# Which token tile gets scattered gates, and in which order the seam asks for its tables: a deal of tiles and two hand-written schedules changed in a decoder layer with expert retrieval

## The chip, the cores and the metric

The kernel runs on one core of one Trainium2 chip. The metric is the device time of one execution in microseconds (us); lower is better. TensorE (PE) does the matrix products, VectorE (DVE) the ranking, the gathered rows and the additions, ScalarE (ACT) copies PSUM out and evaluates activations, GpSimd (POOL) issues the indirect transfers, and SyncE (SP) issues most of the others.

## The reference, cut to what matters

```python
h = concat([meta, x])                                  # 16 + 1024 rows of 1024
proj = rmsnorm(h, norm_mix_g) @ w_in                   # 1024 -> 2048
ya = rmsnorm(pool_mixer(a, pool_w, pool_scale), norm_a_g)
yb = rmsnorm(short_conv_mixer(b_gate, c_gate, val, conv_w), norm_b_g)
h = (h + concat([ya, yb]) @ w_out)[:, 16:]
xf = rmsnorm(h, norm_ffn_g)
# retrieval: 8 heads, 2 x 128 sub-keys, top 16 of each half, top 16 of their sums
idx, gates = peer_retrieve(xf, w_query, sub_keys)      # (1024, 8, 16): expert numbers below 16384
u, v = expert_u[idx], expert_v[idx]
h = h + sum_k gates_k * gelu(u_k . xf) * v_k           # 128 experts for each token
return rmsnorm(h, norm_final_g)
```

## The kernel before

The 1024 tokens are eight tiles of 128. They go through the mixer and the ranking in four groups of two tiles, in the order of `BASE`. A tile's place in that order is its *rank*, 0 to 7. The expert part is then done in two ways:

- Four tiles are **gathered**: for each of 128 choices POOL issues one indirect transfer of 128 rows of 4 KB from `expert_u` (a *row* below, line 626), and DVE takes the dot product (L1122). Later the same is done with `expert_v` (L1133). The rows go through a ring of 8 slots. There are 1024 rows in all, of which the first 256 are the u rows of the first two gathered tiles.
- Four tiles are **dense**: PE multiplies them with all of `expert_u` (`score_tile`, L733, 128 tiles x), ACT applies gelu (L929), DVE multiplies by a table of gates (a *gate* item, L1185), and PE multiplies the result with `expert_v` (L779, 16 groups of 8 pieces), which DVE adds up (a *sum* item, L1191). The tables lie in `g_d`. For three of the dense tiles they are made on chip from one-hot products in 48 batches (`hots`, L1335 and L1339 on DVE, L746 on PE) and stored in chunks (L538). For the fourth, POOL scatters the gates into the table in HBM: 128 indirect transfers, 16 for each of 8 heads (L597). A head's transfers are issued once those of the head before have landed. I call them *scatters*.

The stages follow one another on PE: group n's projections (`bcv`), the output product (`outp`, L691), the turn (L697), the queries and the scores; after group 3 the stage of table batches, with ten score tiles in it and behind it; then the *seam*, where the first sums begin; then the dense stage proper.

The order of DVE's work is written by a small planner. `FILL` gives each slot of a group (behind each convolution, behind `outp`, in the query stage) a budget in us, and `take` fills it with ranking units of the group before (`keys`, `cands`, `pairs`, `digits`, `pick`, `keep`) and with rows of tiles already ranked. `plan["hots", b]` puts rows beside the table batches. What remains is merged with the dense items into `order`: `first_fill` is the place at which gate items begin, and `DENSE_SPEED` their pace. `digits` on DVE releases `pick_places` on ACT (L812, 16 activations), and `pick` waits for it. POOL works through its rows in order, and `head_after` says after which row the scatters of each head stand.

Before, ranks 0, 1, 6 and 7 are gathered, rank 2 is scattered, and ranks 3, 4 and 5 get tables. The scatters stand behind rows 29 (heads 0 and 1), 37 (heads 2 to 4) and 45 (heads 5 to 7). PE's steps don't depend on this deal.

## Time and profile before

| | before |
|---|---|
| median of 3 runs | 2651.85 us (2648.74 to 2654.02) |
| profiled execution, its own time | 2652.4 us |
| its span, first to last instruction | 2650.7 us |
| PE busy | 2509.4 us (95%) |
| DVE busy | 1953.4 us (74%) |
| POOL busy | 1436.2 us (54%) |
| ACT busy | 430.6 us (16%) |
| mean over the span | 324 GB/s |

1.7 us of the profiled time lie outside the span. Times of rows below are counted from the start of the span. "Idle before" in a row is the time for which the engine did nothing ahead of that instruction, and behind the arrow stands who ended it.

### The profile page before, as it was taken

The page shows a single profiled execution, that of the slowest core. Times are in us where ns is not written, and L with a number is a line of the kernel's source. Part 1 is how long each engine was busy: PE and PEld are TensorE (multiplying, and loading weights), DVE is VectorE, ACT ScalarE, POOL GpSimd, SP SyncE. Part 2 cuts the span into 40 slices and gives each one's busy share as a digit, 9 for nine tenths or more (in the row PEclk, how much of TensorE's full clock was granted, in tenths as well). Part 3 has the DMA queues.
Part 4 walks back from the last instruction along what each step waited for, and adds up shares of the span by engine and source line. Part 5 has one row for each costly group of instructions (what it writes and reads, how often), then busy time and mean ns, then how long its engine had stood idle before and what let it go on. Part 6 is the DMA issues. An engine that isn't in the chain of part 4 may idle for free.

```text
span 2650.7 us, 24105 instructions
## 1 busy us (share of the span) xinstructions
PE 2509.4 (95%) x7657; PEld 1380.6 (52%) x7657; DVE 1953.4 (74%) x4210; ACT 430.6 (16%) x790; POOL 1436.2 (54%) x1169
## 2 busy tenths in 40 slices
PE   8999999998878899999999999999999999999993
PEld 7687785876756344444444444444444444444441
DVE  3207678668669788686988867769787687877878
ACT  1212223313678100100010100000000000001010
POOL 0000220678762256676756757657576675666665
PEclk9999999998999899999999999999999999999996
DMA  8543763666589979999999999999999999999998
GB/s 320 188 165 143 296 260 127 191 199 180 134 234 257 363 271 391 348 361 415 381 388 402 383 419 353 389 401 387 419 389 397 384 349 420 391 404 395 371 372 306
DMA packets 285918, 857.88 MB, mean 324 GB/s; under 512 B 41952, under 2 KB 97248, under 8 KB 271200
## 3 DMA queue, kind: packets, MB, share of 16 engines
q0 software_dynamic: 167184, 541.73, 54.8%
q1 hardware_dynamic: 108336, 289.45, 28.9%
q10 hardware_dynamic: 10272, 25.17, 2.4%
q8 instruction: 61, 1.00, 0.1%
q14 instruction: 65, 0.53, 0.1%
HBM read 807.94 MB, written 48.30 MB: 323 GB/s over the span
## 4 chain that ended last, share of the span: by engine, by line
PE 69%; POOL 11%; DVE 7%; DMA 5%; issue 4%; ACT 1%; DVEq 1%; another core or an unknown queue 0%; ACTq 0%; POOLq 0%
PE pairs L779 29%; PE pairs L733 27%; POOL gate_tables L597 8%; PE pairs L646 7%; POOL ring L626 4%; PE pairs L691 3%; DMA ring<-in_expert_u,idx 3%; PE pairs L665 2%; DVE arena L1339 1%; DMA gate_tables<-gate,place 1%; DVE junk L1122 1%; ACT pick_all L812 1%; DMA arena<-gate_tables 1%; PE pairs L658 0%; DVE work L1002 0%
## 5 line engine op out<-in xcount | busy, mean ns | idle before, releaser
L626 POOL DMA_INDIRECT ring<-in_expert_u,idx x512 | 650.8, 1271 | 575.7 <-DVE dots L1122 307.7
L779 PE MATMUL pairs<-arena 128*128 128x512 f32 x2048 | 885.5, 594 | 13.7 <-DVE arena L1185 11.2
L733 PE MATMUL pairs<-arena 128*128 128x512 f32 x2048 | 882.8, 592 | 3.8 <-ACT arena L929 3.8
L1122 DVE CUSTOM_DVE_ANT_0 junk<-ring,xf 128x1024 bf16<-128x1024 f32 x512 | 612.1, 1223 | 182.6 <-DMA ring<-in_expert_u,idx 177.2
L626 POOL DMA_INDIRECT ring<-in_expert_v,idx x512 | 567.0, 1107 | 326.4 <-DVE arena L1133 149.0
L779 PEld LDWEIGHTS pairs<-arena 128*128 128x128 f32 x2048 | 389.8, 191 | 506.9 <-issue 502.3
L733 PEld LDWEIGHTS pairs<-arena 128*128 128x128 f32 x2048 | 388.5, 190 | 490.5 <-issue 490.5
L1133 DVE SCALAR_TENSOR_TENSOR arena<-ring,arena 128x1024 f32<-128x1024 f32 x381 | 473.4, 1283 | 97.4 <-DMA ring<-in_expert_v,idx 92.3
L646 PE MATMUL pairs<-arena 128*128 128x256 f32 (+1 forms) x1792 | 403.3, 388 | 10.9 <-ACT arena L882 9.7
L646 PEld LDWEIGHTS pairs<-arena 128*128 128x128 f32 x1792 | 342.9, 192 | 69.2 <-ACT arena L882 10.3
L597 POOL DMA_INDIRECT gate_tables<-gate,place x128 | 211.7, 1654 | 166.0 <-DVE gate L1141 102.3
L929 ACT ACTIVATE arena<-pairs 128x512 f32<-128x512 f32 x128 | 76.1, 597 | 1197.5 <-PE pairs L733 1018.9
L1133 DVE SCALAR_TENSOR_TENSOR xf<-ring,arena,xf 128x1024 f32<-128x1024 f32 x126 | 155.6, 1283 | 13.9 <-DMA ring<-in_expert_v,idx 13.7
L746 PE MATMUL pairs<-arena 128*128 128x128 f32 x768 | 96.7, 285 | 37.4 <-DVE arena L1339 19.0
L1185 DVE TENSOR_TENSOR arena<-arena 128x512 f32<-128x512 f32 x128 | 87.5, 688 | 60.3 <-ACT arena L929 42.6
L691 PE MATMUL pairs<-arena 128*128 128x512 f32 x256 | 114.3, 605 | 4.0 <-ACT arena L860 4.0
L1191 DVE TENSOR_TENSOR arena<-arena,pairs 128x512 f32<-128x512 f32 x128 | 87.1, 681 | 40.1 <-PE pairs L779 27.9
L746 PEld LDWEIGHTS pairs<-arena 128*128 128x128 f32 x768 | 92.3, 199 | 44.8 <-DVE arena L1339 26.1
L1339 DVE TENSOR_SCALAR arena<-iota,arena 128x128 f32<-128x128 f32 x384 | 101.9, 356 | 8.5 <-PE pairs L746 8.4
L812 ACT ACTIVATE pick_all<-digit,place 128x256 bf16<-128x256 f32 x128 | 80.3, 725 | 81.6 <-DVE digit L1066 81.6
L691 PEld LDWEIGHTS pairs<-arena 128*128 128x128 f32 x256 | 49.5, 194 | 64.2 <-issue 56.6
L998 DVE MAX8 tops<-arena 128x8 f32<-128x128 f32 x112 | 24.5, 280 | 73.2 <-ACT arena L891 71.7
(160 smaller groups left out, 1088.4 us busy)
## 6 DMA issues: line engine op xcount, KB each, us to landing
arena<-in_w_all SPq DMA_DIRECT2D x80, 1024.0 KB
arena<-in_uT SPq DMA_DIRECT2D x128, 512.0 KB
arena<-in_expert_v SPq DMA_DIRECT2D x128, 512.0 KB
arena<-gate_tables SPq DMA_DIRECT2D x32, 1024.0 KB
gate_tables<-arena SPq DMA_DIRECT2D x12, 2048.0 KB
gate_tables<-junk ACTq DMA_DIRECT2D x4, 2048.0 KB, 13.8
ring<-in_expert_u,idx POOLq DMA_INDIRECT x512
ring<-in_expert_v,idx POOLq DMA_INDIRECT x512
```

Of the source, the lines that this page charges most:

```text
L597: nc.gpsimd.indirect_dma_start(out=g_flat, out_offset=bass.IndirectOffsetOnAxis(ap=place[:, k:k + 1], axis=0), in_=gate[:, k:k + 1], in_of ...
L626: nc.gpsimd.indirect_dma_start(out=ring[:, r % RING, :], out_offset=None, in_=expert_u if table == "u" else expert_v, in_offset=bass.Indir ...
L646: last = nc.tensor.matmul(out_, w[:, k, c * P:(c + 1) * P], xn[:, k, :], start=(k == 0), stop=(k == KD - 1))
L691: last = nc.tensor.matmul(pair[:, q * 512:(q + 1) * 512], yT[:, NG * (1 - half) + k, t * P:(t + 1) * P], w_out[q].rearrange("p k n -> p (k ...
L733: last = nc.tensor.matmul(score_bank[x], uslot[:, x % USLOTS, k * P:(k + 1) * P], xfT[:, k, :], start=(k == 0), stop=(k == KD - 1))
L746: last = nc.tensor.matmul(g_bank[(2 * b + m) % 4][:, q * KEYS:(q + 1) * KEYS], hots[:, c, 0, 4 * m + q, :], hots[:, c, 1, 4 * m + q, :], s ...
L779: last = nc.tensor.matmul(o_bank[n % 4], gated[:, x % GSLOTS, t * P:(t + 1) * P], vrows[:, j, half * 512:(half + 1) * 512], start=(j == 0) ...
L812: last = nc.scalar.activation(pick_hot[:, a], digit[:].rearrange("p h s k -> p k (h s)"), ACT.Square, scale=32.0, bias=place16[:, a:a + 1])
L1122: nc.vector.tensor_tensor_reduce(out=junk[:, r % 2, :], in0=row, in1=xf[:, t % 2, :], scale=1.0, scalar=0.0, op0=ALU.mult, op1=ALU.add, ac ...
L1133: nc.vector.scalar_tensor_tensor(out=to[:, k % 2, :], in0=row, scalar=weight[:, k:k + 1], in1=h2 if k == 0 else to[:, k % 2, :], op0=ALU.m ...
L1185: nc.vector.tensor_tensor(s, s, gtab[a // GJ % 2][:, :, a % GJ, :], ALU.mult).then_inc(w_ready, 1)
L1339: last = nc.vector.tensor_scalar(hots[:, c, 1, t, :], iota[:], routeT[:, 1, k:k + 1], routeT[:, 2, k:k + 1], ALU.is_equal, ALU.mult)
```

## The change

Two edits in one. The first deals the ranks out anew: rank 1 is scattered, 0, 3, 6 and 7 are gathered, 2, 4 and 5 get tables. The scatters thus stand behind row 29 (heads 0 to 3) and row 54 (heads 4 to 7), the budgets of `FILL` become one list for each group, and DVE takes 79 rows ahead of the final order, not 60: 22 in group 1, 25 in group 2 (before 8), 16 in group 3 (before 16), and 16 beside table batches (before 14), now from batch 2 on and not from batch 21. The second is about the seam: the last chunk of tables is stored in two transfers, the small first one with what tables 0 and 1 need of it; the load of table 0 waits for the small one only; the additions' starting values are loaded tile by tile ahead of four loads of u; gate items begin after two units of keys and six rows (before: after five units and 14 rows), eight in a row and not ten. `digits` is held back until three sums in a row follow, or until its `pick`.

```diff
-GATHERED_RANK = {0: 0, 1: 1, 6: 2, 7: 3}
-SCATTER_RANK = 2
-DENSE_RANK = {3: 0, 4: 1, 5: 2}
+GATHERED_RANK = {0: 0, 3: 1, 6: 2, 7: 3}
+SCATTER_RANK = 1
+DENSE_RANK = {2: 0, 4: 1, 5: 2}
...
-FILL = (("conv0", 4.0), ("conv1", 4.0), ("conv2", 4.0), ("conv3", 4.0), ("gate", 4.0), ("y", 15.0), ("outp", 10.0), ("query", 68.0))
+FILL = [[(f"conv{g}", 4.0) for g in range(4)] + [("gate", 4.0), ("y", 15.0), ("outp", outp), ("query", query)]
+        for outp, query in ((0.0, 0.0), (10.0, 70.0), (10.0, 72.0), (0.0, 72.0))]
-ROWS_FROM = 20
-FIRST_FILL = 54.0
+FIRST_FILL = 26.0
...
-            plan["hots", b] = take(HOT_FILL) if b >= ROWS_FROM and b % 2 == 1 else []
+            plan["hots", b] = take(HOT_FILL) if b % 3 == 2 else []
...
             if i == first_fill:
-                order += items[:EARLY]
-                done = EARLY
-            order.append(unit)
+                order += items[:VJ]
+                done = VJ
+            if unit[0] == "pick" and held:
+                order.append(held.pop())
+            if unit[0] == "digits":
+                held.append(unit)
+            else:
+                order.append(unit)
+            if held and done + 2 < len(items) and all(k == "sum" for k, _, _ in items[done:done + 3]):
+                order.append(held.pop())
...
-                sp.dma_start(g_d[:, :, FIRST_CHUNK + c, :].rearrange("g p n -> p g n"),
-                             tables[:, c % STAGES].rearrange("p (g j) t -> p g (j t)", j=GJ)).then_inc(table_kept[c % STAGES], 16)
+                if c < TABLE_CHUNKS - 1:
+                    sp.dma_start(to, of).then_inc(table_kept[c % STAGES], 16)
+                else:
+                    sp.dma_start(to[:, 0:2], of[:, 0:2]).then_inc(first_kept, 16)
+                    sp.dma_start(to[:, 2:], of[:, 2:]).then_inc(table_kept[c % STAGES], 16)
...
-            head_after = [scatter_from - 1 + RING * (1 + (h + 1) // 3) for h in range(HEADS)]
+            head_after = [rows_by[1 + 2 * h // HEADS] + RING - 1 for h in range(HEADS)]
```

**On POOL's queue**, from the middle of group 1 up to the table stage (`ring<-in_expert_u` are rows, `gate_tables<-gate` are scatters; the number behind x counts them). Before:

```order
L626 DMA ring<-in_expert_u,idx 128x1024 x30
L597 DMA gate_tables<-gate,place 8388608x1 x32
L626 DMA ring<-in_expert_u,idx 128x1024 x8
L597 DMA gate_tables<-gate,place 8388608x1 x48
L626 DMA ring<-in_expert_u,idx 128x1024 x8
L597 DMA gate_tables<-gate,place 8388608x1 x48
L626 DMA ring<-in_expert_u,idx 128x1024 x82
```

And of the changed kernel:

```order
L651 DMA ring<-in_expert_u,idx 128x1024 x30
L622 DMA gate_tables<-gate,place 8388608x1 x64
L651 DMA ring<-in_expert_u,idx 128x1024 x25
L622 DMA gate_tables<-gate,place 8388608x1 x64
L651 DMA ring<-in_expert_u,idx 128x1024 x73
```

Three blocks of scatters have become two of 64, each followed by rows that DVE takes in the query stage of a group.

**On DVE**, at the end of group 3's ranking and the start of the table stage. Before (`half_i` is the end of the last pick, `gsum` the sums for the gates that PE's first turn of routes waits for, the last two rows are batch 0):

```order
L1080 TENSOR_TENSOR half_i<-pick_all 128x16x8x2
L1101 COPY route<-half_i 128x2x128
L1102 TENSOR_TENSOR route<-best 128x128
L1137 TENSOR_REDUCE gsum<-route 128x8
L1139 RECIPROCAL gsum<-gsum 128x8
L1141 TENSOR_TENSOR route<-route,gsum 128x128
L1335 TENSOR_TENSOR arena<-iota,arena 128x1024
```

And of the changed kernel, where a row is the pair of instructions that reads `ring`, and eight such pairs stand where two are shown first and last:

```order
L1107 TENSOR_TENSOR half_i<-pick_all 128x16x8x2
L1128 COPY route<-half_i 128x2x128
L1129 TENSOR_TENSOR route<-best 128x128
L1149 ISA junk,dots<-ring,xf 128x1024
L1149 ISA dots 128x1
...
L1149 ISA junk,dots<-ring,xf 128x1024
L1149 ISA dots 128x1
L1164 TENSOR_REDUCE gsum<-route 128x8
L1166 RECIPROCAL gsum<-gsum 128x8
L1168 TENSOR_TENSOR route<-route,gsum 128x128
```

Eight rows, 55 to 62, have come in between the last ranking unit and the gates on which the table stage waits.

**On SP's queue** at the seam, from the last chunk of tables on. Before (`gate_tables<-arena` stores, `arena<-gate_tables` loads a table):

```order
L538 DMA gate_tables<-arena 128x32x128
L523 DMA arena<-in_expert_v 128x1024 x3
L528 DMA arena<-gate_tables 128x2048
L523 DMA arena<-in_expert_v 128x1024 x5
L528 DMA arena<-gate_tables 128x2048
L517 DMA arena<-in_uT 128x1024 x4
L554 DMA arena<-h_scratch 128x4x1024
L528 DMA arena<-gate_tables 128x2048 x2
```

And of the changed kernel:

```order
L553 DMA gate_tables<-arena 128x2x128
L554 DMA gate_tables<-arena 128x30x128
L533 DMA arena<-in_expert_v 128x1024 x3
L538 DMA arena<-gate_tables 128x2048
L533 DMA arena<-in_expert_v 128x1024 x5
L538 DMA arena<-gate_tables 128x2048
L575 DMA arena<-h_scratch 128x1024 x4
L527 DMA arena<-in_uT 128x1024 x4
L538 DMA arena<-gate_tables 128x2048 x2
```

The order of the loads of tables and of v is the same; the store is in two, and the starting values stand ahead of the loads of u.

## Rows read from the trace of the kernel before

**Rows 1.** Windows: busy us of PE, PEld, DVE, ACT, POOL; clock, DMA share, GB/s

```profile
1141.00:2604.70 1463.70, 1463.66 (x3410) 647.82 (x3410) 1154.76 (x1480) 92.59 (x149) 964.37 (x825) 1.00 0.99 388
```

**Rows 2.** The chain of work that ended last: start, us, what

```profile
2549.80 54.95 PE pairs L779 x128
```

**Rows 3.** Timeline of DVE, tail: start, us, instruction, operands, count

```profile
2608.48 34.72 DVE L1133 SCALAR_TENSOR_TENSOR xf<-ring,arena,xf 128x1024 f32<-128x1024 f32 x28
```

**Rows 4.** Timeline of PE, groups 2 and 3 and the table stage

```profile
416.82 15.11 PE L691 MATMUL pairs<-arena 128*128 128x512 f32 x28 [3.55 <-ACT arena L860]
...
577.04 13.90 PE L691 MATMUL pairs<-arena 128*128 128x512 f32 x32
...
615.93 1.94 PE L697 MATMUL pairs<-ident,arena 128*128 128x128 f32 x8 [7.80 <-DVE arena L1280]
...
695.29 7.40 PE L746 MATMUL pairs<-arena 128*128 128x128 f32 x48 [4.07 <-DVE arena L1339]
...
737.66 7.03 PE L733 MATMUL pairs<-arena 128*128 128x512 f32 x16
...
764.11 7.03 PE L733 MATMUL pairs<-arena 128*128 128x512 f32 x16
...
802.82 7.03 PE L733 MATMUL pairs<-arena 128*128 128x512 f32 x16
```

**Rows 5.** Timeline of DVE: rows that waited for their transfer, groups 1 and tables

```profile
366.56 1.23 DVE L1122 CUSTOM_DVE_ANT_0 junk<-ring,xf 128x1024 bf16<-128x1024 f32 x1 [2.48 <-DMA ring<-in_expert_u,idx]
...
775.25 1.22 DVE L1122 CUSTOM_DVE_ANT_0 junk<-ring,xf 128x1024 bf16<-128x1024 f32 x1 [15.95 <-DMA ring<-in_expert_u,idx]
```

**Rows 6.** Timeline of POOL: rows (L626) and scatters (L597)

```profile
344.05 1.69 POOL L626 DMA_INDIRECT ring<-in_expert_u,idx  x1 [19.67 <-DVE dots L1122]
346.05 1.99 POOL L626 DMA_INDIRECT ring<-in_expert_u,idx  x1 [0.31 <-issue]
...
355.21 1.49 POOL L626 DMA_INDIRECT ring<-in_expert_u,idx  x1 [0.30 <-issue]
...
368.06 0.95 POOL L626 DMA_INDIRECT ring<-in_expert_u,idx  x1 [1.92 <-DVE dots L1122]
471.28 1.63 POOL L597 DMA_INDIRECT gate_tables<-gate,place  x1 [102.27 <-DVE gate L1141]
...
507.56 2.44 POOL L597 DMA_INDIRECT gate_tables<-gate,place  x1 [5.02 <-DMA gate_tables<-gate,place]
...
768.30 1.00 POOL L626 DMA_INDIRECT ring<-in_expert_u,idx  x1 [0.31 <-issue]
```

**Rows 7.** Page, costliest groups: busy, mean ns of one; idle before

```profile
L597 POOL DMA_INDIRECT gate_tables<-gate,place x128 | 211.7, 1654 | 166.0 <-DVE gate L1141 102.3
```

**Rows 8.** Waits: us in total, times, longest

```profile
POOL gate_tables L597 <- DMA gate_tables<-gate,place: 26.5, 5, 7.5
```

**Rows 9.** Timeline of PE, the seam and the first tiles behind it

```profile
904.83 5.46 PE L779 MATMUL pairs<-arena 128*128 128x512 f32 x6 [11.05 <-DVE arena L1185]
...
1107.14 27.70 PE L733 MATMUL pairs<-arena 128*128 128x512 f32 x64 [3.77 <-ACT arena L929]
```

**Rows 10.** Timeline of DVE at the seam: keys, gates, a sum

```profile
860.48 0.86 DVE L998 MAX8 tops<-arena 128x8 f32<-128x128 f32 x4
...
869.41 0.68 DVE L998 MAX8 tops<-arena 128x8 f32<-128x128 f32 x3
...
906.71 2.50 DVE L1185 TENSOR_TENSOR arena<-arena 128x512 f32<-128x512 f32 x4 [0.19 <-DMA arena<-gate_tables]
923.09 1.30 DVE L1185 TENSOR_TENSOR arena<-arena 128x512 f32<-128x512 f32 x2 [13.88 <-DMA arena<-gate_tables]
...
951.13 0.68 DVE L1191 TENSOR_TENSOR arena<-arena,pairs 128x512 f32<-128x512 f32 x1
```

**Rows 11.** SP's queue at the seam: start, us, transfer

```profile
883.57 0.43 SPq L528 DMA_DIRECT2D arena<-gate_tables  x1
```

**Rows 12.** Windows around the seam's start, columns as in Rows 1

```profile
893.80:912.00 18.20, 7.17 (x10) 3.09 (x11) 14.79 (x50) 2.30 (x3) 6.18 (x5) 0.62 1.02 420
```

More of the change, by code:

```diff
@@ L255, in program @@
         kept = [sem(f"kept{i}") for i in range(GT)]
-        xfT_kept = sem("xfT_kept")
+        xfT_kept = [sem(f"xfT_kept{n}") for n in range(GRPS)]
         keyed = sem("keyed")
@@ L326, in ranking_of, with ranking_of_two @@
                     + [("digits", r, 0), ("pick", r, 0), ("keep", r, 0)])
-        def ranking_of_two(r):
+        def ranking_of_two(r, keys):
             one, two = ranking_of(r), ranking_of(r + 1)
-            return one[:8] + two[:2] + one[8:] + two[2:]
+            return one[:8] + two[:keys] + one[8:] + two[keys:]
         plan, to_rank, ranked = {}, [], set()
-        rows, row_limit, since_digits = 0, 2 * HK, 0.0
+        rows, since_digits = 0, 0.0
         def take(us):
-            nonlocal rows, since_digits, scatter_from, row_limit
+            nonlocal rows, since_digits
             got, spent = [], 0.0
@@ L510, in _ @@
             sp.wait_ge(pe_step, LAST_STEP)
-            sp.wait_ge(xfT_kept, 16 * len(DENSE_GROUP))
+            for n in range(GRPS):
+                if DENSE_OF[n]:
+                    sp.wait_ge(xfT_kept[n], 16 * len(DENSE_OF[n]))
             sp.dma_start(xfT, xfT_d).then_inc(xfT_in, 16)
@@ L549, in _ @@
                 load_v(0, j)
+            stage_kept(last_stage)
             load_gates(1)
+            for t in range(DENSE_TILES):
+                sp.dma_start(sums[:, t, :], of_tile(h2_d, DENSE_TILE[t])).then_inc(d_h2_in, 16)
             while next_u < EARLY + USLOTS:
@@ L572, in _ @@
                 sp.wait_ge(d_out, t + 1)
-                sp.dma_start(of_tile(out, t), sums[:, t, :]).then_inc(out_kept, 16)
+                sp.dma_start(of_tile(out, DENSE_TILE[t]), sums[:, t, :]).then_inc(out_kept, 16)
         @block.gpsimd
@@ L1324, in _ @@
             dve.wait_ge(act_emptied, ACT_STEPS)
-            dve.wait_ge(xfT_kept, 16 * len(DENSE_GROUP))
+            for n in range(GRPS):
+                if DENSE_OF[n]:
+                    dve.wait_ge(xfT_kept[n], 16 * len(DENSE_OF[n]))
             for t in range(GT):
```

67 lines of the change are left out of this document (37 added, 30 removed).

## The prediction

> **What bounds the kernel now.** I read the windows first. From 1141 us to 2604.7 us PE is busy for 1463.66 of 1463.70 us at full granted clock [rows 1], and the chain of waits runs through PE alone up to 2604.75 us [rows 2]. One item, a score tile or a piece of a sum, takes 54.95 / 8 = 6.87 us there. DVE is busy 79% of that stretch and waits for PE. So rows taken out of this stage bring nothing by themselves: their number shows only in the tail, where DVE works off 28 rows that stand behind the last sum, 34.72 us or 1.24 us each [rows 3]. The end is therefore the start of PE's unbroken stretch plus a constant, and what can move is PE's idle time before 1141 us. The timeline of PE shows it, and each stall names who was late:
> - Group 2's output product stalls for 3.55 us because DVE came late from group 1's rows; group 3's turn stalls for 7.80 us [rows 4].
> - The table stage has a steady beat of one score tile and eight batches: 764.11 - 737.66 = 26.45 us. The next beat takes 802.82 - 764.11 = 38.71 us [rows 4]. The reason is on DVE: row 46 came 15.95 us late [rows 5], because POOL issued it at 768.30, behind all scatters [rows 6]. That costs 38.71 - 26.45 = 12.3 us.
> - At the seam PE stands for 11.05 us for the first gate item, and 3.77 us at 1107 us, where ACT's gelu was behind the 16 activations for a `pick` [rows 9].
>
> **The change, part by part.** PE's own instructions are the same. The two new DMA issues on SP and one more on ACT for the tile-wise `xfT` cost some 0.5 us of their queues (0.43 us for one at the seam [rows 11]); I count them at nothing.
>
> *The scatters and the rows behind them.* All of this is POOL's chain, worked out step by step. A scatter takes 1.654 us [rows 7] and 0.3 us to the next; 64 make 125.1 us. Between two heads lies a wait for landing, 26.5 / 5 = 5.3 us [rows 8]; three make 15.9 us. A block of four heads is 141.0 us. The first block starts when row 29 is out: 368.06 + 0.95 [rows 6], plus 1.0 us for the longer `keep` of a scattered rank, so at about 370.3 us, not at 471.28. It ends at 511.3 us, about when the picks of group 2 are done. Then row 30 goes out, and DVE has 17 rows to take. With DVE idle a row's issue takes 0.95 + 0.3 = 1.25 us, and with DVE at rows 1.99 + 0.3 = 2.29 us [rows 6]; the 14 of group 1 took 24.0 us for 13 steps, 1.85 us each. Six at 1.25 and ten at 1.85 put row 46 at 537.3 us. From issue to use it takes 7.0 us in a quiet stretch (768.30 to 775.25) and 11.4 us while weights are loaded (355.21 to 366.56) [rows 5, 6]; I take 9. So group 2's rows end at 547.5 us.
>
> Then row 54 can be issued, and the second block runs from 548.8 to 689.8 us. Behind it stand rows 55 to 62, which DVE must have before the gates that the table stage waits for. The last goes out ten us later (five at 1.25, two at 1.85), lands 7 us after that and is used by 708.0 us; one us for the gates makes 709.0 us. Before, PE had its first routes turned at 691.2 us (695.29 - 4.07 [rows 4]); half a us of that is the turning itself. So the table stage starts **18 us later**: the wait that stood at 759 us has moved to 690 us.
>
> Whether PE or DVE would be later still must be asked. After group 1's rows PE's stall ended 416.82 - 367.8 = 49.0 us behind the last row [rows 4, 5]. From 547.5 that gives 596.5 us in group 3, where PE stood at 577.0 us [rows 4], now 1 us later: up to 18.5 us lost, of which 7.8 us come back, since `keys` and `pick` have left the slot ahead of the turn. PE is ready some 12 us late, at 703 us, still ahead of 709. So that stall is hidden behind POOL's chain; with a quicker POOL it would come out.
>
> *The table stage itself.* Its rows now find a full ring: **-12.3 us**. Two rows more stand there. A beat has 2.7 rows at 1.2 us beside DVE's work for eight batches, which with four rows before took no longer than PE's 26.45, so they are hidden. Only the row in batch 2, where PE is still waiting for DVE at the start (4.07 us [rows 4]), is on the path: **+1.2 us**.
>
> *The seam.* Write P for the shift so far, +6.9 us; the times here are without it. DVE reaches the gate items after two units of keys and six rows, 2 x 8.93 us [rows 10], some 25 us sooner than before, and must now wait for the tables. Table 0 is asked for before the big store lands. Table 1 is not: it was asked for at 883.57 [rows 11] and used at 906.71 [rows 10], 23 us later, in queues full at 420 GB/s [rows 12]. It can't be asked for before about 881. What is ahead of it is the same, but a DVE that waits draws no rows. The bounds are 892 (all of the band for it) and 906.7; I take 898. So gates 4 to 7 are done at 900.5 us. PE, free at 893.8, goes through four products and waits little. But now the units of keys stand between gates and sums: two units, six rows, two gates, one more unit and two rows, 27.7 us with the first sum, and some 1.8 us for table 2, which took 13.88 us of waiting before [rows 10]. First sum at 930; the next three come at 8.4, 8.4 and 9.6 us, each longer than PE's 6.87, so the fourth at 956.4. PE needs one more piece: 963.3 us. Before, it was the third sum at 951.13 + 0.68 [rows 10] and two pieces, 965.5 us. **-2.2 us** only. The 11.05 us are mostly turned into waits for the four sums. Half a clock for some us is in the old figure (0.62 granted in that window [rows 12]) and in mine is hidden behind DVE.
>
> *Digits held back.* The 16 activations now stand where PE is at sums and needs no new gelu: **-3.8 us** [rows 9]. DVE waits some 10 us for them, with 27 us of PE's pieces as cover; without it the 10 us would be PE's.
>
> *The tail.* 27 rows, not 28: **-1.2 us**.
>
> Sum: 18.0 + 1.2 - 12.3 - 2.2 - 3.8 - 1.2 = -0.3 us on the profiled 2652.4 us, which stands 0.5 us above the median of the runs. So about **2651 us**.
>
> **A rule weighed against the trace.** A row's issue takes 0.95 us with DVE idle and 1.99 us with DVE at rows [rows 6]. The Trainium skill, "SBUF — State Buffer", section "SBUF: two separate sides", says that a DVE operation with two SBUF inputs and a GpSimd operation that reads SBUF take a shared port pair in turns, and the later one stands until the other is done. By that rule all rows behind DVE's would cost the long price; the trace has a mean of 1.85, since DVE itself often waits for a row. By the one the sum is as above, by the other it is the rival D below.
>
> **The rivals.**
> - *A, as forecast*: the scatters' wait moves ahead and eats what the table stage gives. 2651 us. For it: the same 128 scatters at a fixed rate, and rows behind them in front of the gates.
> - *B, POOL is quicker*: landing waits of half the size and rows that land in 7 us. The first block saves 8, the rows 2; group 2's rows end at 537.5 us, the second block at 672 us, and POOL is no longer late. PE's own stall is then 537.5 + 49.0 - 578 = 8.5 less 7.8 us, and DVE's ranking, with one unit and one pick more in the query slot, some us: +5 for +18. The time is 2638 us. Against it: five waits with a mean of 5.3 us.
> - *C, the seam gives what it promises*: table 1 at 892 and no wait for table 2: first sum at 922, PE hardly stands, and the seam gives 10 us, not 2.2. 2643 us. Against it: the band was full.
> - *D, slower*: every row of the two runs behind the scatters is issued at 2.29 us and lands in 11.4. Group 2's rows end 4.4 + 2.4 = 6.8 us later, the last of group 3 another 0.9 + 4.4 us. The table stage starts 18 + 12 = 30 us late. 2663 us. It decides from a start about 24 us late.
>
> **How the numbers follow.** What a measurement of this kernel can tell from no change is about 0.2%, 5.3 us. A has 0.38, B 0.26, C 0.15, D 0.21. A lies inside the 5.3 us on both sides, so: faster 0.40 (B, most of C), same 0.38, slower 0.22. The range takes B and C in and D up to its nearer part: 2636 to 2662 us. Within A alone it is 2646 to 2657 us.
>
> **What the profile of the changed kernel would show.** POOL: scatters in two blocks, from about 370 to 511 and from 549 to 690 us. PE: a stall of ten us or more at group 3's output product, none of 7.8 us at its turn, then some ten us ahead of the turn of routes, waiting for DVE's gates, and there DVE waiting for rows. In the table stage, every beat 26.45 us. At the seam no idle of 11 us, but short waits for DVE's sums (L1191 before), 5 us at the first. No 3.77 us in the tiles behind group 1. A tail 1.2 us shorter. I am wrong if POOL's second block ends before 675 us, or if gates 4 to 7 are done well before 900 us on the old clock.

## The result, and the profile after

| | before | changed |
|---|---|---|
| median of the runs, us | 2653.81 | 2660.59 |
| fastest and slowest run, us | 2644.22, 2657.03 | 2655.36, 2668.75 |
| runs | 11 | 11 |

The ratio is 1.0033, with a 95% interval of 1.0023 to 1.0043: the change makes the kernel slower by a third of a per cent, 8.8 us. (The medians in the table are 6.8 us apart and the means 9.0; 8.8 is the ratio applied to the median of before.) The ratios leave out slow executions, of which there was one (6661 us, of the kernel with 51 early rows below). The profiled execution of the changed kernel took 2665.74 us (span 2664.0), 13.3 us over that of before. A second profile of it in a later group of runs had a span of 2656.7 us; the ratio there was 1.0044 (1.003 to 1.0058).

Windows of the changed kernel over the stretch of [rows 1], columns as there:

```profile
1141.00:2604.70 1463.70, 1457.12 (x3391) 644.82 (x3390) 1130.32 (x1455) 101.50 (x163) 947.55 (x803) 1.00 0.97 380
```

PE is still busy nearly throughout, but 6.5 us less than in [rows 1]: there is a stall that was not there before. The chain of waits again ends with PE alone, and the last piece starts 14.5 us later than in [rows 2]:

```profile
2564.30 54.95 PE pairs L804 x128
```

So the loss arose earlier. PE's timeline, with the places of [rows 4] and [rows 9] and some new ones (L804 is the sum, L779 before; L758 the score tile, L733 before; L771 the table batch, L746 before; L716 the output product, L691 before; L671 the query, L646 before):

```profile
15.90 17.89 PE L690 MATMUL pairs<-arena 128*128 128x272 f32 x64 [3.21 <-DVE arena L1236]
...
303.19 1.19 PE L671 MATMUL pairs<-arena 128*128 128x256 f32 x2 [10.10 <-ACT arena L907]
...
476.57 2.05 PE L671 MATMUL pairs<-arena 128*128 128x256 f32 x4 [4.59 <-ACT arena L907]
...
599.09 3.52 PE L716 MATMUL pairs<-arena 128*128 128x512 f32 x4 [2.71 <-ACT arena L885]
...
712.50 0.87 PE L748 MATMUL pairs<-ident,route 128*128 128x128 f32 x3 [10.07 <-issue]
717.44 7.64 PE L771 MATMUL pairs<-arena 128*128 128x128 f32 x48 [4.07 <-DVE arena L1368]
...
761.26 7.03 PE L758 MATMUL pairs<-arena 128*128 128x512 f32 x16
...
787.69 7.03 PE L758 MATMUL pairs<-arena 128*128 128x512 f32 x16
...
877.44 27.63 PE L758 MATMUL pairs<-arena 128*128 128x512 f32 x64
...
975.90 55.10 PE L758 MATMUL pairs<-arena 128*128 128x512 f32 x128
...
1140.70 27.63 PE L804 MATMUL pairs<-arena 128*128 128x512 f32 x64
1174.91 29.79 PE L804 MATMUL pairs<-arena 128*128 128x512 f32 x64 [6.58 <-DVE arena L1218]
1204.53 5.74 PE L758 MATMUL pairs<-arena 128*128 128x512 f32 x13
```

The same rows of before that [rows 4] lacks:

```profile
14.93 14.90 PE L665 MATMUL pairs<-arena 128*128 128x272 f32 x64 [3.21 <-DVE arena L1209]
...
866.15 27.63 PE L733 MATMUL pairs<-arena 128*128 128x512 f32 x64
...
1134.69 6.17 PE L779 MATMUL pairs<-arena 128*128 128x512 f32 x14
...
1190.04 10.46 PE L733 MATMUL pairs<-arena 128*128 128x512 f32 x24
```

In before, the first score tile behind the seam starts at 965.70 us, group 2's sums at 1134.69 and the tiles behind them at 1190.04; in the change these are 975.90, 1140.70 and 1204.53. Read by stages, against the forecast's terms:

| stretch | forecast, us | profiles, us |
|---|---|---|
| start of the tables | +18.0 | 717.44 - 695.29 = +22.2 |
| table stage | 1.2 - 12.3 = -11.1 | (877.44 - 717.44) - (866.15 - 695.29) = -10.9 |
| seam, to the first whole score tile | -2.2 | (975.90 - 877.44) - (965.70 - 866.15) = -1.1 |
| tiles behind group 1 | -3.8 | (1140.70 - 975.90) - (1134.69 - 965.70) = -4.2 |
| sums of group 2 | 0 | (1204.53 - 1140.70) - (1190.04 - 1134.69) = +8.5 |
| tail, behind PE's last piece | -1.2 | 13.3 - 14.5 = -1.2 |

These make the +13.3 of the two profiled executions. Some 4 us of the first line are no effect of the change: 64 matmuls at 15.90 us took 17.89 us where the same ones of before took 14.90, and group 0's scores, ahead of all that the change moves, begin at 188.98 us against 185.12. The change's second profile has 16.59 us there, and its tables start at 710.98 us. With these 4 us out, the 13.3 become about 9, and the runs say 8.8. The first line has one more disturbance, on the other side. Ahead of group 1's query the profile of before stands 5.97 us, of which some 3 are a wait of ACT for which it names no engine ("3.22 <-remote" at 291.14 below); the profiles of the kernels further down that store behind both copies have 1.7 to 2.3 us at this place. The first profile of the change has such a wait too (3.17 us at 294.95), its second has not. Counted from group 0's first query, the tables start 695.29 - 128.43 = 566.9 us on in before, and 717.44 - 132.28 = 585.2 and 710.98 - 129.72 = 581.3 us on in the two profiles of the change. So the line is +14 to +18 us with the start taken out.

Two new stalls stand out, and the profile shows the cause of each. The first is on ACT, at the end of group 1's turns. L907 copies a turn to the buffer that PE's query reads; L911 stores the transposed tile, L872 and L873 store two others. Columns: start, us, instruction.

```profile
294.95 1.02 ACT L907 ACTIVATE arena<-pairs 128x1024 f32<-128x1024 f32 x1 [3.17 <-remote]
296.01 0.55 ACTq L911 DMA_DIRECT2D xfT_scratch<-arena  x1
296.59 0.85 ACTq L872 DMA_DIRECT2D h_scratch<-arena  x1
297.47 4.55 ACTq L873 DMA_DIRECT2D xf_scratch<-arena  x1
302.07 1.02 ACT L907 ACTIVATE arena<-pairs 128x1024 f32<-128x1024 f32 x1 [6.09 <-issue]
```

The copy of the second turn starts 6.09 us after ACT could have had it, and what fills the time are three issues on its own queue, one of them of 4.55 us. The stores of h and xf stand between the two copies in the kernel before as well. But there they are issued while the first copy runs; only the store of the transposed tiles, which waits for a copy to end, stands behind both:

```profile
291.14 1.02 ACT L882 ACTIVATE arena<-pairs 128x1024 f32<-128x1024 f32 x1 [3.22 <-remote]
291.15 0.33 ACTq L847 DMA_DIRECT2D h_scratch<-arena  x1
291.51 0.53 ACTq L848 DMA_DIRECT2D xf_scratch<-arena  x1
294.08 1.02 ACT L882 ACTIVATE arena<-pairs 128x1024 f32<-128x1024 f32 x1 [1.91 <-remote]
295.13 0.59 ACTq L886 DMA_DIRECT2D xfT_scratch<-arena  x1
```

Five more profiles, of kernels below that keep this order of stores, have 10.24 to 10.52 us ahead of group 1's query. There the first copy has no such wait, and the stores of h and xf behind the transposed tile take 1.31 to 1.66 and 6.58 to 7.04 us. In group 2 they take 1.43 to 1.81 and 0.53 to 0.84 us in all six.

The second is on DVE, in the sums of group 2 (L1149 is a row, L1092 and L1093 the end of the digits, L1099 the start of the pick, L1218 a sum):

```profile
1147.02 1.23 DVE L1149 CUSTOM_DVE_ANT_0 junk<-ring,xf 128x1024 bf16<-128x1024 f32 x1 [1.28 <-DMA ring<-in_expert_u,idx]
...
1151.82 0.28 DVE L1093 TENSOR_TENSOR digit<-pos,pick_all 128x128 f32<-128x128 uint32 x1
1162.12 2.29 DVE L1099 TENSOR_TENSOR pick_all<-topf,pick_all 128x4096 bf16<-128x4096 bf16 x1 [10.02 <-ACT pick_all L837]
...
1174.17 0.69 DVE L1218 TENSOR_TENSOR arena<-arena,pairs 128x512 f32<-128x512 f32 x1
```

The digits end at 1152.1, DVE waits 10.02 us for ACT's 16 activations, and behind the waiting pick stand two rows, a gate, three rows and the first sum. PE has nothing to do without that sum: it stands for 6.58 us, and the 64 matmuls behind the stall take 29.79 us instead of 27.63.

### The profile page after: what moved, and what is told of

Read it like the earlier page. It is cut to its first block, busy times and chain, and to the rows that moved or that the text cites. A ratio compares the mean times of both kernels' runs of the same rounds, so it can differ in the third digit from the quotient of the medians.

```text
span 2664.0 us, 24115 instructions
## 1 busy us (share of the span) xinstructions
PE 2521.2 (95%) x7657; PEld 1388.3 (52%) x7657; DVE 1954.5 (73%) x4210; ACT 430.1 (16%) x790; POOL 1430.7 (54%) x1169
## 4 chain that ended last, share of the span: by engine, by line
PE 69%; POOL 11%; DMA 7%; issue 5%; DVE 4%; ACT 3%; ACTq 1%; DVEq 0%; another core or an unknown queue 0%; POOLq 0%; SPq 0%
PE pairs L804 28%; PE pairs L758 28%; POOL gate_tables L622 7%; PE pairs L671 7%; DMA ring<-in_expert_u,idx 4%; POOL ring L651 4%; PE pairs L716 2%; PE pairs L690 2%; DMA gate_tables<-gate,place 1%; ACT arena L948 1%; PE pairs L771 1%; ACT arena L972 1%; DVE junk L1149 1%; ACT pick_all L837 1%; DMA arena<-gate_tables 1%
## 5 line engine op out<-in xcount | busy, mean ns | idle before, releaser
L651 POOL DMA_INDIRECT ring<-in_expert_u,idx x512 | 636.1, 1242 | 685.8 <-DVE dots L1149 410.0
L804 PE MATMUL pairs<-arena 128*128 128x512 f32 x2048 | 891.0, 597 | 15.3 <-DVE arena L1218 12.0
L758 PE MATMUL pairs<-arena 128*128 128x512 f32 x2048 | 882.5, 592 | 0.0
L651 POOL DMA_INDIRECT ring<-in_expert_v,idx x512 | 578.7, 1130 | 330.0 <-DVE arena L1160 166.4
L1149 DVE CUSTOM_DVE_ANT_0 junk<-ring,xf 128x1024 bf16<-128x1024 f32 x512 | 613.4, 1224 | 179.8 <-DMA ring<-in_expert_u,idx 165.7
L804 PEld LDWEIGHTS pairs<-arena 128*128 128x128 f32 x2048 | 391.7, 192 | 512.2 <-issue 496.4
L758 PEld LDWEIGHTS pairs<-arena 128*128 128x128 f32 x2048 | 388.6, 190 | 486.5 <-issue 486.5
L671 PE MATMUL pairs<-arena 128*128 128x256 f32 (+1 forms) x1792 | 406.5, 390 | 18.3 <-ACT arena L907 16.5
L671 PEld LDWEIGHTS pairs<-arena 128*128 128x128 f32 x1792 | 344.9, 193 | 77.6 <-ACT arena L907 17.1
L1218 DVE TENSOR_TENSOR arena<-arena,pairs 128x512 f32<-128x512 f32 x128 | 87.2, 682 | 49.9 <-PE pairs L804 32.2
L771 PE MATMUL pairs<-arena 128*128 128x128 f32 x768 | 94.0, 282 | 28.9 <-ACT arena L972 22.8
L716 PE MATMUL pairs<-arena 128*128 128x512 f32 x256 | 114.9, 607 | 5.1 <-ACT arena L885 5.1
L771 PEld LDWEIGHTS pairs<-arena 128*128 128x128 f32 x768 | 91.1, 197 | 34.8 <-issue 24.5
L716 PEld LDWEIGHTS pairs<-arena 128*128 128x128 f32 x256 | 49.7, 195 | 65.6 <-issue 56.1
```

The lines of the kernel that those rows point to most:

```text
L651: nc.gpsimd.indirect_dma_start(out=ring[:, r % RING, :], out_offset=None, in_=expert_u if table == "u" else expert_v, in_offset=bass.Indir ...
L671: last = nc.tensor.matmul(out_, w[:, k, c * P:(c + 1) * P], xn[:, k, :], start=(k == 0), stop=(k == KD - 1))
L716: last = nc.tensor.matmul(pair[:, q * 512:(q + 1) * 512], yT[:, NG * (1 - half) + k, t * P:(t + 1) * P], w_out[q].rearrange("p k n -> p (k ...
L758: last = nc.tensor.matmul(score_bank[x], uslot[:, x % USLOTS, k * P:(k + 1) * P], xfT[:, k, :], start=(k == 0), stop=(k == KD - 1))
L771: last = nc.tensor.matmul(g_bank[(2 * b + m) % 4][:, q * KEYS:(q + 1) * KEYS], hots[:, c, 0, 4 * m + q, :], hots[:, c, 1, 4 * m + q, :], s ...
L804: last = nc.tensor.matmul(o_bank[n % 4], gated[:, x % GSLOTS, t * P:(t + 1) * P], vrows[:, j, half * 512:(half + 1) * 512], start=(j == 0) ...
```

## The experiments

My theory after the result: the loss is these two waits. The forecast had seen both instructions, had counted the stores at nothing and the wait of the pick as covered by other work. The rivals: the later start of the tables is a matter of POOL's chain, as forecast; or the early rows are not worth what they cost. In all runs the ratio is to the kernel before, measured on the same chip and in the same group of runs. The change itself came out at 1.0033 above and at 1.0044 in the last group, so a difference of 0.1% across groups says nothing.

**The two edits apart.** The first kernel has the new deal of ranks alone, with the seam's instructions as before; the second the old deal with the seam's edit.

> The first edit alone: the new deal of tiles, POOL's two blocks of scatters, the new budgets and rows beside table batches, with the seam, the start of the gate items and the place of digits as before. Theory: this edit is itself a loss. In the changed kernel's profile the table stage ended at 877.4 us, before at 866.2; some 4 us of these 11 are a slower start of that one execution (the same instructions of group 0 ended 4 us later), 7 us are the edit's. The 3.77 us at the tiles behind group 1 come back, so nothing is gained later but a row in the tail. Ratio to before 1.002 to 1.003, table stage ended some 7 us later. Rival, as I forecast it: the deal gives nothing and takes 6.9 us less 1.2, ratio 1.002, by the rows behind the scatters alone and without a gap ahead of the queries of groups 1 and 2. The profile tells these apart: by the theory the gap ahead of group 1's query is over 8 us (before 5.97), by the rival 6. A second rival, that the edit is free and only that one profile was slow: ratio 1.000.

> The second edit alone, on the deal of before: the last chunk stored in two, table 0 asked for first, starting values tile by tile, gate items after six rows and eight in a row, digits held back. In this order digits of rank 6 stands one row ahead of its pick, right before group 2's sums. Theory: holding digits back is a loss where the pick follows at once, since DVE comes to it late from rows that wait for their transfers; DVE then waits some 10 us and PE 5 to 7 us for the first sum of group 2. The 3.77 us gap goes, the seam gives 1 to 3 us: ratio 1.000 to 1.002. Rival, as forecast: the wait is covered by PE's pieces, and the edit gains 2.2 + 3.8 + some tenths: ratio 0.9975.

The deal alone: 1.0015 (1.0007 to 1.0024). The seam alone: 1.0018 (1.0009 to 1.0027). Each costs half, and together they make the change's 0.33%. The query gap of group 1 is 10.24 us with the deal alone and 1.86 us with the seam alone; the stall in the sums of group 2 is absent from the first and 8.94 us in the second, at 1160.35. So each new stall belongs to one edit: the stores to the deal, the pick to the seam.

**Each wait taken out of the change.**

```diff
-            if unit[0] == "pick" and held:
-                order.append(held.pop())
-            if unit[0] == "digits":
+            if unit[0] == "digits" or (held and unit[0] == "pick"):
                 held.append(unit)
...
+                order.append(held.pop(0))
+                released = done
+            elif held and held[0][0] == "pick" and done >= released + 2:
+                order.append(held.pop(0))
```

> The changed kernel with one thing mended: digits of rank 6 is held until sums follow, and its pick is held too, until two sums have gone by, so that DVE has rows and sums to do while ACT makes the 16 activations. Theory: PE's idle 6.58 us at the fifth piece of group 2 and the half clock behind it (29.8 us for 64 instructions that take 27.5) go away, about 8.5 us: ratio to before 1.000 to 1.001, against 1.0033 of the changed kernel, and no PE idle in the sums of group 2. Rival: DVE is late there because its rows wait for transfers, not because of the pick; then moving the pick gives under 3 us, ratio 1.0022 or more.

```diff
-                    if GT * n + i in DENSE_PLACE:
+                    if i == GT - 1 and DENSE_OF[n]:
                         act.wait_ge(act_emptied, empty((kind, n, i)))
...
+                        for j in range(GT):
+                            if GT * n + j in DENSE_PLACE:
```

> The changed kernel with ACT's stores of the transposed tile issued behind both turns of the group, as before the change, and not behind each. Theory: in group 1 the store of the first turned tile stands ahead of the two stores of the second tile and of the copy that the queries wait for; this costs 4.1 us in group 1 (PE idle 10.10 us, before 5.97) and 2.7 us in group 2 (4.59, before 1.86). If PE is what the table stage waits for, ratio 1.001; the gaps are 6 and 2 us in the profile. Rival: the table stage waits for POOL's chain and the rows behind it; then the gaps close as well but the time stays, ratio 1.003, and PE waits the longer ahead of the turn of routes.

The pick two sums later: 1.0008 (0.9994 to 1.0021), and no stall in the sums of group 2, where two sums stand between the digits and the pick. The stores behind both turns: 1.0004 (0.9992 to 1.0015); the query gaps are 1.78 and 1.84 us. Each edit undoes about what it should. But with the stores moved, group 3's output product stands for 8.89 us at 580.28, where it stood for 2.71 in the change. A good part of the gain went into the next wait, behind DVE's rows.

**Both out; and the seam alone, mended.** In these two and in all kernels that follow with the pick later, the condition is `unit[0] == "pick" and (held or done < released + 2)`, so that a pick met shortly behind the release of its digits is held too.

> The change with both suspected costs taken out: DVE's pick stands two sums behind the digits, and the stores of the gated tiles' transposed rows stand on ACT's queue behind both turns' copies. Nothing is left out of the computation. Theory (the change's loss is these two waits, and the rest of the forecast's sum holds): the gaps ahead of the queries fall from about 10 and 4.5 us to about 2 and 2, the 8.5 us stall in group 2's sums is gone, and the seam's gain stays; beside the change alone that is 8 to 14 us less, a ratio of 0.997 to 0.999 to the kernel before. First rival (what ends the stretch ahead of the tables is the chain of POOL's blocks, so that the queries' gaps cost nothing): only the pick's share comes back, ratio 0.999 to 1.001. Second rival (the loss is one that neither edit touches, the later start of the tables): 1.002 or more.

> The kernel before, with the seam's edit alone (gates asked for first, the stage's copy in two pieces) and with the pick held until two sums stand between the digits and it. The deal of the tiles is that of before. Theory (the seam's edit gives what its terms say, 2.2 us at the seam and 3.8 us in batch 1, and the seam alone came out slow because of the stall of about 9 us that the pick causes in the sums): 6 to 11 us under the seam alone, a ratio of 0.996 to 0.999. Rival (the seam's edit moves time from one wait to the next whatever the order of the pick): 1.000 to 1.002, with a stall of 4 us or more somewhere in group 2's stretch.

Both out: 0.9963 (0.995 to 0.9977), better than either theory gave it, and faster than the kernel before. The seam alone with a later pick: 0.9976 (0.9967 to 0.9985), which is 0.42% under the same without it (across two groups of runs). The forecast's two terms for the seam and the tiles, -2.2 and -3.8 us, would make 0.9977 by themselves. So the seam's edit was good, and the place of one instruction of it cost more than it brought. The two mendings together bring 0.70% from the change (1.0033 to 0.9963) and singly 0.25% and 0.29%; that is across two groups of runs, and whether they help each other isn't shown.

**The rows ahead of the gates.** In both kernels group 3 has eight rows fewer, those between the last pick and the gates:

```diff
-        for outp, query in ((0.0, 0.0), (10.0, 70.0), (10.0, 72.0), (0.0, 72.0))]
+        for outp, query in ((0.0, 0.0), (10.0, 70.0), (10.0, 72.0), (0.0, 60.0))]
```

> The change with both suspected costs taken out, and with the gates no longer behind the last rows of group 3: those 12 rows' share is set so that the rows stand behind the gates. Theory (PE's own path ends beside POOL's, since the last score's copy and the last gated tile's load come at 711 us and the tables' first matmul at 712): under 3 us less than the same kernel with the rows ahead of the gates. Rival (the forecast's: the gates wait for the rows, and the tables for the gates): 8 to 15 us less, the tables' first matmul at 700 or earlier.

> The change itself, with nothing undone but the eight rows that stand between the last pick and the gates of group 3: they are left for later (71 early rows, not 79), all else as in the change. Forecast's chain (in the change the tables wait for the gates, the gates for these rows, the rows for POOL's second block): the tables begin 8 us or more sooner, and the kernel is 0.15% or more under the change of the same call. Rival (PE's own path, made late by ACT's queue and by group 2's rows, ends at the same time): the tables begin within 4 us of where they begin in the change, and the time is within 0.1% of it.

> The change itself once more, for its own time in this call and for a second profile. Both theories: 1.002 to 1.0045 to the kernel before, the query gaps at 10 and 4.5 us and the stall of 6 to 7 us in the sums of group 2 again. What is open is the first profile's 10.07 us ahead of the turn of routes, for which it names no releaser: if the tables waited for the gates behind the rows, this profile shows the turn released by DVE; if the wait was PE's own, it is under 4 us here, with the tables' start at about 710 us.

Without the two waits: 0.996 (0.9947 to 0.9973) beside 0.9963, no difference. In the change itself: 1.0055 (1.0042 to 1.0069) beside 1.0044 (1.003 to 1.0058), no gain either. The tables begin at 705.84 us without these rows and at 710.98 with them, but 3.0 us of these were there at the turn already (631.11 against 634.11), so the rows cost 2.1 us there. And in this kernel the stall at the pick has grown to 9.74 us, from 6.11:

```profile
1164.67 30.42 PE L804 MATMUL pairs<-arena 128*128 128x512 f32 x64 [9.74 <-DVE arena L1218]
```

The turn of routes in the change, second profile, and without the rows:

```profile
706.01 0.90 PE L748 MATMUL pairs<-ident,route 128*128 128x128 f32 x3 [3.14 <-DVE route L1168]
```

```profile
701.24 0.53 PE L748 MATMUL pairs<-ident,route 128*128 128x128 f32 x3 [1.26 <-ACT arena L916]
```

The tables do wait for the gates behind POOL's rows, as forecast, but in this profile by 2 us. In the first profile PE was ready at 702.43 us and DVE's gates were done at 708.56, half a us from the forecast's 709.0, so 6.1 of the 10.07 us are the gates' there too. The rest is ACT: its last two copies of scores (L916) waited 2.00 and 5.46 us with "<-remote" for a releaser, the last ran from 711.33 to 712.35, and the turn started at 712.50. What ACT waited for is open; in the second profile the last copy is at 702.96.

**Fewer early rows.** The kernel with both waits out, and with 58 rows ahead of the final order (12 in group 2, 8 in group 3), not 79. The kernel before has 60.

```diff
-        for outp, query in ((0.0, 0.0), (10.0, 70.0), (10.0, 72.0), (0.0, 72.0))]
+        for outp, query in ((0.0, 0.0), (10.0, 70.0), (10.0, 54.0), (0.0, 60.0))]
```

> The change with both suspected costs taken out, and with fewer early rows: 12 in group 2's stretch and 8 in group 3's, 58 in all, where the change has some 70. Nothing is left out of the computation. Theory of the forecast (the chain on POOL, whose second block waits for group 2's rows, is what the tables wait for): the second block begins 15 to 20 us sooner, the tables begin at 690 to 700 instead of 709, the rows left over return as waits in the table stage where POOL writes one in 11 to 12 us and PE needs one in 9 to 10; ratio 0.996 to 0.999, within 0.1% of the same kernel with all the rows. Rival (early rows are worth their full price, since the table stage is bound by rows): 5 to 15 us more than the same kernel with all the rows. Second rival (rows early are pure delay): 10 to 18 us less.

0.992 (0.9907 to 0.9932): the second rival, rows early as pure delay. It is the largest step of all, 0.43% under the same kernel with 79 rows. PE at group 3's output product with 79 rows:

```profile
583.38 3.75 PE L718 MATMUL pairs<-arena 128*128 128x512 f32 x4 [12.22 <-ACT arena L887]
```

and with 58 (from the second run of that kernel, below), where it does not stand:

```profile
569.04 13.90 PE L718 MATMUL pairs<-arena 128*128 128x512 f32 x32
582.77 3.62 PE L708 MATMUL pairs<-arena,ones 128*128 128x256 f32 x16
```

With 79 rows DVE took its last row of group 2, and then began the pooling of group 3, here:

```profile
543.63 1.23 DVE L1153 CUSTOM_DVE_ANT_0 junk<-ring,xf 128x1024 bf16<-128x1024 f32 x1
544.78 0.08 DVE L1153 DVE_READ_ACCUMULATOR2_ANT dots<- 128x1 f32 x1
544.78 0.44 DVE L1250 TENSOR_TENSOR arena<-arena 128x271 f32<-128x271 f32 x1
```

and with 58 rows here:

```profile
515.99 1.22 DVE L1153 CUSTOM_DVE_ANT_0 junk<-ring,xf 128x1024 bf16<-128x1024 f32 x1 [2.24 <-DMA ring<-in_expert_u,idx]
517.14 0.08 DVE L1153 DVE_READ_ACCUMULATOR2_ANT dots<- 128x1 f32 x1
517.14 0.43 DVE L1250 TENSOR_TENSOR arena<-arena 128x271 f32<-128x271 f32 x1
```

27.6 us apart, of which 2.0 are in the executions already at group 2's query (461.35 against 459.39): 25.6 us for 13 rows, of which 16 are the rows themselves (1.23 us each) and the rest longer waits for transfers. 12.2 us of it reach PE as this stall. The tables start 18.6 and 20.9 us sooner (700.39 against 681.75 and 679.50 in the two profiles with 58 rows), but the runs gain 11: in the first of these profiles 7 us are given back between the start of the tables and the end (1942.9 us against 1935.8), where exactly is not traced. And the row stall of [rows 5] does not come back, though fewer rows are early than in the kernel before. PE's beats in the table stage of this kernel:

```profile
723.48 7.03 PE L760 MATMUL pairs<-arena 128*128 128x512 f32 x16
...
749.92 7.03 PE L760 MATMUL pairs<-arena 128*128 128x512 f32 x16
...
776.35 7.03 PE L760 MATMUL pairs<-arena 128*128 128x512 f32 x16
```

26.4 us each. The stall of before was there because a block of scatters ran into the table stage ([rows 6], the row at 768.30); in the new deal the last scatter is out by 658 us. It is the order of the scatters that removes it, and the rows were not needed for it.

**Which rows.** Three kernels beside each other: eight rows of group 3 put back, `(10.0, 54.0), (0.0, 72.0)`; fewer still, `(10.0, 44.0), (0.0, 50.0)`, 51 early; and the 58 once more.

> The kernel with both suspected costs taken out and 12 rows in group 2's stretch, but with group 3's 8 rows behind the last pick and ahead of the gates put back (66 early rows). If the loss was in group 2's rows, which push DVE's work for group 3 and let PE wait 12 us for it: the tables begin within 8 us of where they begin with 58 rows, ratio 0.991 to 0.993. Rival (the rows ahead of the gates are what the tables wait for, as the forecast's chain has it): the tables begin 12 to 18 us later, ratio 0.995 to 0.997.

> The kernel with both suspected costs taken out, and with 51 early rows: 8 in group 2's stretch and 5 in group 3's. Theory (with 58 rows PE has no wait of over 4 us left ahead of the tables, so that nothing is left to gain there): the tables begin within 2 us of where they begin with 58 rows, and the seven rows more that are left for later cost 0 to 6 us, ratio 0.992 to 0.994. Rival (each early row costs as much as it did between 79 and 58, 0.6 us): 3 to 5 us less than with 58 rows, ratio 0.990 to 0.991.

> The kernel with 58 early rows once more, beside the two that differ from it by rows alone: ratio 0.991 to 0.993, as in its first run. The place of the others is read against this run and not against the first, since runs of one call share the chip and the runs of the kernel before.

0.9915 (0.9897 to 0.9933), 0.992 (0.9899 to 0.9941) and 0.9929 (0.9911 to 0.9947), in this order: no difference between the three. So the step came from group 2's 13 rows alone, group 3's eight are free here, and below 58 nothing more is to be had. The tables start at 681.04 us with 51 rows, at 679.50 and 681.75 with 58, and at 686.82 with group 3's rows put back; those 7.3 us were there at group 3's turn already (611.86 against 604.76), ahead of the rows in question, and PE waits only 1.26 us at the turn of routes, for ACT.

**The rows alone.** The change with 58 early rows and neither wait removed:

> The change with nothing else undone: the pick right behind the digits and the stores of the transposed rows in the turns, as in the change, but 58 early rows in place of 79 (13 fewer in group 2's stretch, 8 fewer in group 3's). Theory (early rows on DVE's queue in group 2 and behind the last pick in group 3 are a cost of the change's own, of the same size with the two waits as without them): 7 to 12 us under the change alone, a ratio of 0.999 to 1.001 to the kernel before. Rival (the two waits hide it: the chain on POOL is as late as the rows, since it is fed late): no more than 4 us under the change alone, 1.002 to 1.003.

1.0018 (1.0005 to 1.003), 0.15 to 0.26% under the change of the other groups of runs; the rival's value rather than the theory's. The tables start at 695.01 us, 16 us before those of the change's second profile, and 7 of these are lost again at the pick:

```profile
1156.83 29.49 PE L804 MATMUL pairs<-arena 128*128 128x512 f32 x64 [12.93 <-DVE arena L1218]
```

12.93 us where the change has 6.58 and 6.11. My reading is that DVE comes to the digits with the rows that were not taken early still ahead of it. Three kernels with the change's rule for the pick bear it out: with 79, 71 and 58 early rows the last cast of the digits (L1092) starts 10.8 (10.4 in the second profile), 16.4 and 22.4 us behind PE's first piece of group 2, and PE then stands 6.58 (6.11), 9.74 and 12.93 us. So an early row is worth something as long as the pick stands there, and this also hides what taking fewer rows gives at the tables. With the pick later there is no such stall, and the same 21 rows fewer bring 0.43%.

## Why the prediction was wrong

The forecast was 2651 us with -0.3 us as the sum; measured were +8.8. Slower had a chance of 0.22, the least of the three, and the time of 2660.59 lies in the range, near its end. The rival D, 2663 us, was nearest in time but not in its reason: POOL's work was hardly slower than assumed where it was slower at all. The first block of scatters took 377.30 to 520.04, 142.7 us for the forecast's 141.0, the second 557.33 to 690.82, 133.5. The 25 row issues between them took 1.06 us on average, and while DVE was at rows back to back (from 548.64 to 554.8) most took 0.94: "1.99 with DVE at rows" did not come back. Row 55 was in use 4.2 us after its issue (691.12 to 695.35). D's sum was wrong as well. With "every row" at 2.29 us, the ones counted at 1.25 too, it gives 13.0 + 10.5 us, a start 41 us late and 2674 us.

By the terms of the sum, the 8.8 us are the sums of group 2 (0 forecast, +8.5). The cost of the stores lies within the start of the tables, where a POOL chain that was forecast too late made room for it.

- **The step that failed first: "I count them at nothing"**, the DMA issues for the tile-wise `xfT`. I priced the issue by its own time, 0.43 us, on SP. (The count was short too: `xfT` is stored four times and not twice, and at the seam SP issues four transfers more.) On ACT it stands between the copies of two turns and waits for the first to end, so the two stores of the second tile, which were issued during that copy before, now come behind it and ahead of the second copy; one of them took 4.55 us. That made 10.10 - 1.9 = 8.2 us in group 1 and 4.59 - 1.8 = 2.8 us in group 2, against gaps of 1.86 and 1.79 us in the seam alone, where the store follows both copies (before's own profile has 5.97 and 1.86). Its worth in the time is 0.29% from the change alone (1.0033 to 1.0004) and, across two groups of runs, 0.45% with the pick out as well (1.0008 to 0.9963).
- **The second: the cover for the digits.** "DVE waits some 10 us for them, with 27 us of PE's pieces as cover." The wait was 10.02 us and the -3.8 us came (-4.2). But it was checked at group 1's digits only. In group 2's the pick stands ahead of the first sum, with only five rows and a gate between, DVE itself was late, and PE stood: +8.5 us. Moving the pick is worth 0.25% from the change and, across two groups of runs, 0.42% in the seam alone.
- **The start of the tables, +18.0**, came out at about that size (22.2 less 4; +14 in the second profile), but by luck: two errors cancel. The forecast had the second block from 548.8 to 689.8. Where the stores don't delay the turns, it ran from 543.33 to 675.21: it began 5.5 us sooner and, since its waits for landing were 1.8, 3.7 and 1.7 us and not 5.3 each, took 131.9 us and not 141.0. The tables started at 698.31; counted from group 0's first query that is 1.4 us behind the profile of before and 9.4 us behind that of the seam's edit alone (568.3, 566.9 and 558.9 us). In the change the two query gaps moved the whole chain back: block from 557.33. The figure of 703 us for PE's own path was met (702.4 and 702.9 in the change), but again not by its reason: it had in it a stall at the output product that was mostly not there, and not the gaps that were. Nor was that path simply hidden. With the stores moved the turn of routes waited for the gates by 1.76 us and with both waits out by 4.38, of which 1.26 is what it waits for ACT without the rows: the two paths end within about 3 us of each other, and group 2's rows push both.
- **The stall at group 3's output product**, "ten us or more", was 2.71 and 4.42 us in the change, as PE itself was late there, and 12.22 us with both waits out. It was the largest price of the early rows, and I had named it and put it behind POOL's chain.
- **The table stage** (-11.1, measured -10.9), **the seam** (-2.2, measured -1.1: short waits of 2.57, 3.14 and 2.28 us for a gate and the sums in place of 11.05) and **the tail** (-1.2, measured -1.2) held, the seam at half its size. With the shift of 11.3 us (22.2 - 10.9) taken off, gates 4 to 7 were done at 902.4 us and the first sum began at 929.1, for 900.5 and 930 in the forecast.

What is left of the parts: the seam with a later pick is worth -0.24%, and the full kernel with both waits out and 58 rows is at 0.9920 and 0.9929 in its two runs, some 20 us under the kernel before. What of that is the deal's own can be read from one group of runs: the old deal with the mended seam and its 60 early rows is at 0.9976, the new deal with both waits out at 0.9963 with 79 rows and at 0.992 with 58. So at about the same number of early rows the deal is worth 0.56%, some 15 us, of which 79 rows leave 0.13%. The old deal was not tried with its rows placed otherwise.

## What to carry to other kernels

Price a moved or added DMA issue by what stands behind it on its engine, and not by its own length: here a store of 0.55 us between two copies that PE waits for cost PE 8 us. When an instruction is held back for its cover, check the cover at every place where the rule applies, and see that the one who waits for its result does not stand in front of another engine's work. And before filling an engine with early work, ask which edit removed the stall that the early work was meant for: here the order of the scatters did, and the rows added with it cost 0.4% once the two waits were out, and about 0.2% while they stood.

## What the runs showed of the hardware

- An issue of a plain store of h or xf on ACT's queue took 0.33 to 1.01 us at the turns of groups 1 and 2 where no store of the transposed tile stood ahead of it (four of them within 2.4 us from 289.11, in the kernel with the stores moved). Behind such a store, the first took 0.85 to 1.81 us and the second 4.55 to 7.04 us in group 1 but 0.53 to 0.84 in group 2. Two stores of a transposed tile right behind one another took 4.7 to 5.3 us together, where one took 0.5. What makes such an issue wait is not shown.
- The wait for landing between heads of scatters varies much: five waits with a sum of 26.5 us before [rows 8], and in the change six with 24.6:

```profile
POOL gate_tables L622 <- DMA gate_tables<-gate,place: 24.6, 6, 7.2
```

while a block of 64 scatters in one of the kernels (both waits out, 79 rows) ran from 547.37 to 676.52 us, 129.2 us in all, of which the scatters by themselves are 125. Over all runs of the new deal a block of 64 took 129.1 to 143.8 us. A chain that has three such waits in it should be given with some 15 us of play.
- After 6.58 us of standing PE's next 64 matmuls took 29.79 us instead of 27.63; the granted clock was 1.00 up to the stall, 0.59 in the 5.1 us behind it (between the levels of 1.2 and 2.4 GHz) and 1.00 again from 1180 us. Over the stalls of 6.11 to 12.93 us at this place the extra was 1.9 to 3.0 us, and it didn't grow with their length.
- The same instructions ahead of the change's first effect took 3 to 4 us more in one profile than in others, so that a difference of two profiled executions must be read from a point behind it.
